# Modulation columns moved between the products of one token tile, first-layer splits moved to GpSimd, one subtraction moved in the recurrence

## The chip, the cores and the metric

The kernel runs on one core of a Trainium2 chip. The metric is the device time of one launch in microseconds (us). Time before: median 1755.17 us of three runs, 1753.87 to 1757.62.

## The reference

Two blocks of two layers each, on 512 tokens of width 1024, all in float32:

```python
def first_block(x, c, ...):
    c_act = jax.nn.silu(c)
    for i in range(DEPTH):                      # 2
        mods = jnp.split(c_act @ w_ada[i] + b_ada[i], 6, axis=-1)
        sh1, sc1, g1, sh2, sc2, g2 = [m[:, None, :] for m in mods]
        u = x * (1.0 + sc1) + sh1
        y = gla_mixer(...) if i % 2 == 0 else chunk_attention(...)
        x = layer_norm(DEEPNORM_ALPHA * x + (1.0 + g1) * y, ln_g[i, 0], ln_b[i, 0])
        u = x * (1.0 + sc2) + sh2
        y = squared_relu_mlp(u, ff_w1[i], ff_w2[i])      # square(relu(u @ w1)) @ w2, inner width 4096
        x = layer_norm(DEEPNORM_ALPHA * x + (1.0 + g2) * y, ln_g[i, 1], ln_b[i, 1])
    return x

def second_block(x, c, ...):
    cond = jax.nn.silu(c)
    for l in range(DEPTH):                      # 2
        mod = cond @ ada_w[l] + ada_b[l]
        shift, scale, gate = jnp.split(mod, 3, axis=-1)
        h = rms_norm(x, norm_g[l]) * (1.0 + scale[:, None, :]) + shift[:, None, :]
        y = even_mixer(...) if l % 2 == 0 else odd_mixer(...)
        x = x + gate[:, None, :] * y
    return x
```

The modulation of each block (`c_act @ w_ada`, `cond @ ada_w`) is computed from the vector `c` while the layers before it run. `even_mixer` begins with a product with `even_w_in`, then runs a recurrence with four heads (`hgrn2_chunked`) beside a pooled branch.

## The kernel before

**Products.** Each float32 operand is held as a high part (rounded to fp32r) and a low part (the rest), and each product is three matmuls: high by high, high by low, low by high (`PASSES`; `pe_tile`, L234, for the products with the transposed input `xT`; `down_tile`, L538, for the second feed-forward product). `xT[:, 0]` is the high part of the input, `xT[:, 1]` the low part. A half panel of weights (4 blocks of 128 rows by 512 columns) is loaded into `raw` by SyncE (SP), rounded into the high part by ScalarE (`act_high`, L191 and L192), and the low part is subtracted by GpSimd (`low`, L2595), block by block. PE waits for each block of the low part (`low_ready`).

**The token stream.** Tokens are in four tiles of 128. At a stage's end VectorE (DVE) mixes product, gate and residual for a tile; ScalarE normalises it; PE turns it (transposes, `pe_transposes_by_tile`, L375) into 8 PSUM banks; ScalarE writes `u` and the high part of `xT` (L416, L417); DVE subtracts the low part (`dve_split_x`, L423).

**The start.** DVE multiplies and adds `w_ada` in four groups of eight pieces (`first_tile`, L2716 and L2718) as SP brings them. After each group PE adds up the columns (`pe_first_columns`, L310 and L312), and ScalarE writes two blocks of `xT` with them. PE therefore takes the first panel block by block: products of block k, and after k = 0, 2, 4 the turning of the next two blocks of `x` (`pe_first_x`, L298) and their columns. DVE's splits of blocks 0 to 5 stand between its `first_tile` pieces; 6 and 7 stand behind them. `pe_at_work` (L304) is a run of matmuls whose result nobody reads.

**The end of the second feed-forward (`pe_ff`, `dve_ff` with l = 1).** The last two inner blocks are done as a pair (`down_pair`): output columns 0 to 511 (n = 0) into banks 4 to 7, then columns 512 to 1023 (n = 1) into banks 0 to 3, tile by tile, each tile with twelve matmuls of `hT` and twelve of `xT`. The modulation of the second block is ready in `modacc` by then, spread over partitions; it is added up by PE: as rows (`pe_modrow`, L776, for the two gates) or as columns (`pe_modcols`, L770: one matmul with one output column per 128 entries; the trace shows two records for each). In n = 1, tile 0, columns 0 to 15 stand one by one ahead of the first sixteen of the 24 matmuls. Columns 24 to 39 stand behind the rows, after the last product. On DVE `add_pair(n, t)` is add the earlier sum (L703), gate (L704), residual (L705), statistics (L819); a tile that was settled before (`settle`, L691 and L692: gate and residual of the earlier sum) skips the add. Ahead of the first tile of n = 1 stands `before_pair`: it waits for the columns (`mod_done` at 9) and makes the scale and shift of the next stage (L2758, L2781 to L2783). Behind the four tiles stand L2758 for columns 24 to 39 and `next_rows` (L2776, four pieces), and then `mod_made` goes to 9. PE turns banks 0 to 2 ahead (tiles 0 to 2), does three idle matmuls (L384), turns tile 3 of blocks 0 to 2, and waits for `mod_made` at 9 before it touches bank 3, which holds columns 24 to 39, and banks 4 to 7, which hold the rows.

**The recurrence (`hgrn_dve`).** One loop over 28 + 3 steps on DVE: `diff(t)` prepares an exponent for ScalarE (L2306, L2307), `take`, `gate`, `scaled(t - 1)` uses it (L2317, L2318), and at every sixth step `ends`, `states` (seven short dependent instructions, L2355 and L2357) and `written`.

The order on every engine is the order of the code; semaphores tie the engines together.

## Time and profile before

| | |
|---|---|
| median of three runs | 1755.17 us |
| the profiled execution, time | 1757.64 us |
| its span | 1755.8 us |
| granted TensorE clock, mean of the span | 0.995 |
| PE busy | 1739.7 us (99%) |
| PEld (weight load) busy | 1446.9 us (82%) |
| DVE busy | 1055.2 us (60%) |
| ACT busy | 765.2 us (44%) |
| POOL busy | 783.3 us (45%) |

Between the profiled execution's own time and its span lie 1.84 us. The chain of work that ended last runs on PE for 92% of the span, on DVE for 4%. Times within the span are given from its start. A row of the timeline has start, length, engine, line, operation, output and inputs, shapes, and count; in brackets the idle time of the engine before it and what ended it. Several like instructions are merged in a row; a matmul's end is modelled and reaches over the start of the next.

### The profile page before, as it was taken

To read this page: it belongs to the slowest core of one execution; us is meant where nothing else is said; L and a number is where in the kernel's file an instruction comes from. 1 tells how busy PE (TensorE), PEld (TensorE's weight loads), DVE (VectorE), ACT (ScalarE), POOL (GpSimd) and SP (SyncE) were. 2 spreads that over 40 slices of the span, in tenths; PEclk is the share of its full clock that TensorE was granted. 3 is DMA by queue.
4 is the path that set the end of the run, shared out by engine and by line. 5 is a ranking of instruction groups with operands and counts; after the bars stand their busy time and mean duration, and the time that the engine had idled before them with its cause. 6 is when DMAs were issued, how large, how long until landed. Compare 5 with 4: busy or idle time off the path is not lost.

```text
span 1755.8 us, 24977 instructions
## 1 busy us (share of the span) xinstructions
PE 1739.7 (99%) x9169; PEld 1446.9 (82%) x9169; DVE 1055.2 (60%) x1627; ACT 765.2 (44%) x1313; POOL 783.3 (45%) x610
## 2 busy tenths in 40 slices
PE   8999999999999999999999999999999999999999
PEld 7777788888888878888888888888888888888887
DVE  6887565666665862653465666659377844336752
ACT  3444445222222264663532222233545457666660
POOL 4524145555555464232355555553532344353342
PEclk9999999999999999999999999999999999999999
DMA  9744326645555233222285555541221122324521
GB/s 318 264 155 153 127 96 228 212 157 172 169 168 185 98 120 108 85 73 73 72 286 172 171 171 170 171 157 67 96 96 55 49 98 72 110 89 136 153 91 72
DMA packets 133884, 242.09 MB, mean 138 GB/s; under 512 B 6896, under 2 KB 44912, under 8 KB 133792
## 3 DMA queue, kind: packets, MB, share of 16 engines
q1 hardware_dynamic: 131616, 236.64, 41.4%
q10 hardware_dynamic: 2176, 4.19, 0.7%
q8 instruction: 61, 1.00, 0.2%
q14 instruction: 31, 0.25, 0.0%
HBM read 238.68 MB, written 2.13 MB: 137 GB/s over the span
## 4 chain that ended last, share of the span: by engine, by line
PE 92%; DVE 4%; DMA 1%; ACT 1%; issue 1%; SPq 0%; POOL 0%; DVEq 0%; POOLq 0%; ACTq 0%
PE bank L234 48%; PE bank L538 20%; PE bank L1536 5%; PE bank L1502 4%; PE bank L1504 3%; PE bank L1616 2%; PE bank L1604 2%; PE bank L1578 2%; DMA ring_s<-in_first_ada 1%; PE bank L2109 1%; PE bank L770 1%; PE bank L1095 0%; PE bank L1109 0%; DMA ct<-cumd 0%; PE bank L1840 0%
## 5 line engine op out<-in xcount | busy, mean ns | idle before, releaser
L2595 POOL TENSOR_TENSOR wsp<-raw,wsp 128x512 fp32r<-128x512 f32 x528 | 762.2, 1476 | 886.7 <-ACT wsp L191 886.7
L234 PE MATMUL bank<-xT,wsp 128*128 128x512 f32 x2592 | 601.5, 391 | 5.1 <-POOL wsp L2595 2.5
L234 PEld LDWEIGHTS bank<-xT,wsp 128*128 128x128 f32 x2592 | 486.2, 188 | 110.8 <-DVE xT L423 3.4
L191 ACT ACTIVATE wsp<-raw 128x1024 fp32r<-128x1024 f32 x132 | 139.8, 1059 | 485.6 <-PE bank L538 238.3
L538 PE MATMUL bank<-wsp,hT 128*128 128x512 f32 x1344 | 310.7, 390 | 0.0
L234 PE MATMUL bank<-wsp,xT 128*128 128x512 f32 x1248 | 299.4, 395 | 0.6 <-DVE xT L423 0.3
L538 PEld LDWEIGHTS bank<-wsp,hT 128*128 128x128 f32 x1344 | 252.3, 188 | 51.8
L234 PEld LDWEIGHTS bank<-wsp,xT 128*128 128x128 f32 x1248 | 230.7, 188 | 52.6 <-issue 4.9
L192 ACT ACTIVATE wsp<-raw 128x1024 fp32r<-128x1024 f32 x132 | 138.1, 1046 | 0.0
L685 DVE TENSOR_TENSOR x<-bank,x 128x512 f32<-128x512 f32 x80 | 55.0, 688 | 100.0 <-PE bank L538 100.0
L763 DVE SCALAR_TENSOR_TENSOR modacc<-ada_ring,csil,modacc 128x768 f32<-128x768 f32 (+1 forms) x80 | 99.4, 1243 | 4.0 <-DMA ada_ring<-in_ada_w 0.5
L669 DVE TENSOR_TENSOR hT<-h,hT 128x512 fp32r<-128x512 f32 x56 | 80.1, 1488 | 24.7 <-ACT hT L619 24.7
L1502 PE MATMUL bank<-xT,wsp 128*128 128x512 f32 x384 | 93.6, 397 | 0.0
L658 DVE TENSOR_TENSOR h<-bank,h 128x512 f32<-128x512 f32 x64 | 43.3, 687 | 75.7 <-ACT h L614 75.7
L614 ACT ACTIVATE h<-bank 128x512 f32<-128x512 f32 x64 | 38.3, 599 | 112.9 <-PE bank L234 112.9
L423 DVE TENSOR_TENSOR xT<-u,xT 128x512 fp32r<-128x512 f32 x64 | 53.7, 848 | 55.4 <-ACT xT L417 54.9
L1502 PEld LDWEIGHTS bank<-xT,wsp 128*128 128x128 f32 x384 | 70.4, 188 | 16.1 <-issue 2.0
L1709 DVE CUSTOM_DVE_ANT_0 aP<-bank,abt 128x512 f32<-128x512 f32 (+3 forms) x64 | 27.0, 487 | 69.4 <-PE bank L1578 59.8
L763 DVE SCALAR_TENSOR_TENSOR tok<-ring,csil,tok 128x512 f32<-128x512 f32 x56 | 54.9, 980 | 9.8 <-DMA ring<-in_w_ada 4.5
L763 DVE SCALAR_TENSOR_TENSOR modacc<-u,csil,modacc 128x768 f32<-128x768 f32 (+1 forms) x32 | 52.9, 1652 | 2.4 <-DVE modacc L763 0.5
L1504 PE MATMUL bank<-wsp,xT 128*128 128x256 f32 x384 | 48.0, 285 | 0.0
L1504 PEld LDWEIGHTS bank<-wsp,xT 128*128 128x128 f32 x384 | 46.5, 192 | 0.7 <-issue 0.7
(330 smaller groups left out, 2029.8 us busy)
## 6 DMA issues: line engine op xcount, KB each, us to landing
raw<-in_ff_w SPq DMA_DIRECT2D x64, 1024.0 KB, 5.4
ada_ring<-in_w_ada SPq DMA_DIRECT2D x48, 384.0 KB, 3.8
ada_ring<-in_ada_w SPq DMA_DIRECT2D x48, 384.0 KB, 3.7
ring<-in_w_ada SPq DMA_DIRECT2D x64, 256.0 KB, 3.1
raw<-in_odd_w_in SPq DMA_DIRECT2D x16, 1024.0 KB, 5.5
raw<-in_gla_w_in SPq DMA_DIRECT2D x12, 1024.0 KB, 6.7
raw<-in_att_w_in SPq DMA_DIRECT2D x12, 1024.0 KB, 5.2
raw<-in_even_w_in SPq DMA_DIRECT2D x12, 1024.0 KB, 5.2
```

What stands on the lines that cost most here:

```text
L191: act.activation(wsp[:, slot, 0, 0:HK // 2], raw[:, slot, 0:HK // 2], ACT.Copy).then_inc(hi_part, 1)
L192: act.activation(wsp[:, slot, 0, HK // 2:HK], raw[:, slot, HK // 2:HK], ACT.Copy).then_inc(hi_made, 1)
L234: mm = pe.matmul(out_ap, l, r, start=(start and n == 0), stop=(stop and n == 2))
L423: dve.tensor_tensor(xT[:, 1, k], u32[:, k % 2], xT[:, 0, k].bitcast(F32), ALU.subtract)\
L538: mm = pe.matmul(bank[bk][:, :], h[:, a, k, t * P:t * P + P], wsp[:, slot, c, k, :], start=(start and k == 0 and q == 0), stop=(stop and k ...
L669: dve.tensor_tensor(h[:, 1, t], h32[l][:, t], h[:, 0, t].bitcast(F32), ALU.subtract)\
L685: ins = dve.tensor_tensor(y, bank[4 + t][:, :], y, ALU.add)
L763: ins = dve.scalar_tensor_tensor(acc, w, c, acc, ALU.mult, ALU.add)
L1502: mm = pe.matmul(bank[D_BANK][:, :], w[:, i * P:i * P + P], xT[:, a, k, :], start=start, stop=stop)
L1504: mm = pe.matmul(bank[D_BANK][:, side:side + COLS // 2], xT[:, a, k, i * P:i * P + P], w, start=start, stop=stop)
L1536: mm = pe.matmul(bank[4 * n + t][:, :], (o_hi, o_lo)[a][name][:, kk, t * P:t * P + P], wsp[:, h, b, k, :], start=(kk == 0 and q == 0), sto ...
L2595: ins = pool.tensor_tensor(wsp[:, slot, 1, k], raw[:, slot, k], wsp[:, slot, 0, k].bitcast(F32), ALU.subtract)
```

## The change

1. The modulation columns 24 to 39 of the second feed-forward's end go from behind the rows to between the products of n = 1, tile 0: twelve matmuls of `hT` now carry columns 0 to 15, twelve of `xT` carry columns 24 to 39, one or two ahead of each. One signal (`mod_done`) stands behind the last of them. DVE takes both sets in `before_pair`.
2. PE turns four blocks ahead (k = 0 to 3) there, with eight idle matmuls, where it was three and three.
3. DVE settles tiles 3, 2 and 1 between its four squares, where it settled tile 3 behind its modulation pieces; `add_pair(1, 1)` and `add_pair(1, 2)` lose their add.
4. At the start the splits of `xT` blocks 0 to 5 go from DVE to GpSimd, between its low parts of the weights. For blocks 0 and 1 PE does all eight matmuls with the high part first, then the four with the low part.
5. `pe_at_work` 24 becomes 30, 6 becomes 10, 3 and 2, with waits for the first weights' high part and for `u` of block 0 between.
6. In the recurrence `diff(13)`, `diff(19)` and `diff(25)` stand one step earlier, ahead of `states`.

```diff
@@ -533,8 +533,8 @@
                         low_ready(pe, j, k)
                     for q, (a, c) in enumerate(PASSES):
                         n = 3 * k + q
-                        if n < len(columns):
-                            pe_modcols(pe, modacc[l], columns[n:n + 1], ST, mod_done if columns[n] == 15 else None)
+                        if columns:
+                            pe_modcols(pe, modacc[l], columns[n::3 * HK], ST, mod_done if columns[n] == 35 else None)
                         mm = pe.matmul(bank[bk][:, :], h[:, a, k, t * P:t * P + P], wsp[:, slot, c, k, :],
                                        start=(start and k == 0 and q == 0), stop=(stop and k == HK - 1 and q == 2))
                 return mm
@@ -577,7 +577,7 @@
                         if q == 0:
                             pe.wait_ge(s["ada_used"], KT * FB)
                             pe.wait_ge(s["acc_done"], 8 * i + 1)
-                        columns = (range(12), range(12, 16))[q]
+                        columns = (range(16), range(24, 40))[q]
                     mm = down_tile((hT[l], xT)[q], j + 2 + q, q, t, t, q == 0, q == 1, columns)
                     if t == ST - 1:
                         mm.then_inc(w_used, 1)
@@ -597,8 +597,6 @@
                 pe.wait_ge(s["acc_done"], 8 * (FB - 2) + 2 * r + 2)
                 pe_modrow(pe, modacc[l], off, ST + 2 * r, mod_done)
             pe.wait_ge(s["acc_done"], 8 * (FB - 2) + 2 * ST)
-            if l:
-                pe_modcols(pe, modacc[l], range(24, 40), HK - 1, mod_done, at=SEQ - P)
 
         def act_ff(act, l):
             s = FS[f"ff{l}"]
@@ -740,16 +738,20 @@
             for i in range(ST + 1, FB - 2):
                 step(i)
             ada(FB - 1, range(0, 4))
-            square(FB - 1)
+            for t in range(ST):
+                square(FB - 1, [t])
+                if affine and t < ST - 1:
+                    settle(1, ST - 1 - t)
             low(FB - 1, xT)
             ada(FB - 1, range(4, 8))
-            settle(1, ST - 1)
+            if not affine:
+                settle(1, ST - 1)
             for t in range(ST):
                 add_pair(0, t)
             for t in range(ST):
                 if t == (0 if affine else 2):
                     before_pair()
-                add_pair(1, t, t == ST - 1)
+                add_pair(1, t, t == ST - 1 or affine and t > 0)
                 if affine:
                     affine(t)
 
@@ -1114,7 +1116,15 @@
             for k in range(KT):
                 low_ready(pe, base["gla_in"] + k // HK, k % HK)
                 pe.wait_ge(free, k + 1)
-                for t in range(ST):
+                if k < 2:
+                    for a in range(2):
+                        if a:
+                            pe.wait_ge(ts["xT_ready"], ts["k0"] + k + 1)
+                        for t in range(ST):
+                            for b in range(2 - a):
+                                mm = pe.matmul(bank[t][:, :], wsp[:, 0, b, k, t * P:t * P + P], xT[:, a, k, :],
+                                               start=(k == 0 and a == 0 and b == 0), stop=False)
+                for t in range(ST if k >= 2 else 0):
                     mm = pe_tile(pe, bank[t][:, :], k // HK, k % HK, k, t, "T", k == 0, k == KT - 1,
                                  (ts["xT_ready"], ts["k0"] + k + 1) if t == 0 else None)
                     if k == KT - 1 and t < ST - 1:
@@ -2394,7 +2404,7 @@
                 dve.tensor_tensor(y, y, hu[:, t], ALU.mult).then_inc(s["pout"], 1)
 
             for t in range(NI + 3):
-                if t < NI and scaled_number(t) is not None:
+                if t < NI and scaled_number(t) is not None and not (t > 12 and t % 6 == 1):
                     diff(t)
                 if t >= 3:
                     take(t - 3)
@@ -2408,6 +2418,8 @@
                 if t >= 6 and t % 6 == 0 and t // 6 <= 4:
                     ends(t // 6 - 1)
                 if t >= 12 and t % 6 == 0:
+                    if t + 1 < NI:
+                        diff(t + 1)
                     states(t // 6 - 2)
                 if t >= 18 and t % 6 == 0:
                     written(t // 6 - 3)
@@ -2594,8 +2606,32 @@
                         pool.wait_ge(hi_made, 2 * i + slot + 1)
                     ins = pool.tensor_tensor(wsp[:, slot, 1, k], raw[:, slot, k], wsp[:, slot, 0, k].bitcast(F32), ALU.subtract)
                     ins.then_inc(lo_part if k < HK - 1 else lo_made, 1)
+            def low_of(slot, k):
+
+                ins = pool.tensor_tensor(wsp[:, slot, 1, k], raw[:, slot, k], wsp[:, slot, 0, k].bitcast(F32), ALU.subtract)
+                ins.then_inc(lo_part if k < HK - 1 else lo_made, 1)
+
+            def split_x(k):
+
+                ts = TS["in_gla_in"]
+                pool.wait_ge(ts["u_made"], ts["k0"] + k + 1)
+                pool.wait_ge(ts["bank_free"], k + 1)
+                pool.tensor_tensor(xT[:, 1, k], u32[:, k % 2], xT[:, 0, k].bitcast(F32), ALU.subtract).then_inc(ts["xT_ready"], 1)
+
+            pool.wait_ge(hi_made, 1)
+            for k in range(HK):
+                low_of(0, k)
+                if k < 2:
+                    split_x(k)
+            for k in (2, 3):
+                split_x(k)
+            pool.wait_ge(hi_made, 2)
+            for k in range(HK):
+                low_of(1, k)
+                if k < 2:
+                    split_x(HK + k)
             first = base["odd_in"] // 2 + PHASE0["odd_in"]
-            with pool.Fori(0, first) as i:
+            with pool.Fori(1, first) as i:
                 for slot in range(2):
                     low(i, slot)
             low(first, 0)
@@ -2675,11 +2711,15 @@
             for t in range(NV):
                 mm = pe.transpose(bank[0][:, t * P:t * P + P], vrow[:, t, :], ident[:, :])
             mm.then_inc(vtr_done, 1)
-            pe_at_work(pe, 24)
+            pe_at_work(pe, 30)
             pe.wait_ge(cols_made, 1)
             pe_first_x(pe, 0)
             pe_first_columns(pe, 0)
-            pe_at_work(pe, 6)
+            pe_at_work(pe, 10)
+            pe.wait_ge(hi_made, 1)
+            pe_at_work(pe, 3)
+            pe.wait_ge(TS["in_gla_in"]["u_made"], TS["in_gla_in"]["k0"] + 1)
+            pe_at_work(pe, 2)
             gla_pe(pe)
             pe_panels(pe, "gla_out", "mid_gla_out", [("NN", 1)], begin=pe_first_half_gla)
             pe_transposes_by_tile(pe, "hid_ff0", 2, KT - 1, idle=8)
@@ -2690,7 +2730,7 @@
             pe_out(pe, a_sem, "att_out")
             pe_transposes_by_tile(pe, "hid_ff1", 1, KT - 1, idle=8)
             pe_ff(pe, 1)
-            pe_transposes_by_tile(pe, "in_even_in", 1, HK - 1, lambda: pe.wait_ge(mod_made, 9), idle=3)
+            pe_transposes_by_tile(pe, "in_even_in", 1, HK, lambda: pe.wait_ge(mod_made, 9), idle=8)
             pe_panels(pe, "even_in", "in_even_in", [("TT", 1)])
             hgrn_pe(pe)
             pe_transposes_hgrn(pe, range(KT - 1))
@@ -2725,11 +2765,8 @@
             for g in range(HK):
                 for k in range(KT):
                     first_tile(g, k)
-                    if g and k == 3:
-                        dve_split_x(dve, "in_gla_in", 2 * g - 2)
-                    elif g and k == 5:
-                        dve_split_x(dve, "in_gla_in", 2 * g - 1)
             dve.sem_inc(mod_made, 1)
+            dve.wait_ge(TS["in_gla_in"]["xT_ready"], TS["in_gla_in"]["k0"] + KT - 2)
             for k in range(KT - 2, KT):
                 dve_split_x(dve, "in_gla_in", k)
 
@@ -2816,6 +2853,7 @@
 
             def before_pair1():
                 next_columns(0, ST, col("ada_b_2", 0, 16), 9)
+                next_columns(24, ST, col("ada_b_2", 24, 16), 9)
                 rms_fold(0)
                 dve.sem_inc(mod_made, 1)
                 dve.wait_ge(ln_ld, 128)
@@ -2827,7 +2865,6 @@
                 dve.scalar_tensor_tensor(x[:, t], tok[:, t], rstd[:, t:t + 1], lnrow[1][:, 1], ALU.mult, ALU.add)\
                    .then_inc(RS["even_in"]["x"], 1)
             dve_ff(dve, 1, KT, DEPTH, gate2, 96, before_pair1, affine1)
-            next_columns(24, HK - 1, col("ada_b_2", 24, 16), 12, SEQ - P)
             next_rows(1, 0.0, 10)
             dve.sem_inc(x_new, 1)
             dve_transposed(dve, "in_even_in")
```

The end of the second feed-forward on PE; L538 are products, L776 the rows, L770 the columns, L375 turns, L384 idle matmuls, L234 the next stage's products. Before:

```order
L538 MATMUL bank<-wsp,xT 128x512 x12
L776 MATMUL bank<-modacc,ones 128x512 x4
L770 MATMUL bank<-ones,modacc 128x1 x16
L375 MATMUL bank<-ident,tok 128x128 x9
L384 MATMUL bank<-ident 128x128 x3
L375 MATMUL bank<-ident,tok 128x128 x23
L234 MATMUL bank<-xT,wsp 128x512 x192
```

And now (L778 the rows):

```order
L538 MATMUL bank<-wsp,xT 128x512 x12
L778 MATMUL bank<-modacc,ones 128x512 x4
L375 MATMUL bank<-ident,tok 128x128 x12
L384 MATMUL bank<-ident 128x128 x8
L375 MATMUL bank<-ident,tok 128x128 x20
L234 MATMUL bank<-xT,wsp 128x512 x192
```

The sixteen columns are gone from here, three more turns are ahead, and five more idle matmuls.

The last squares of the second feed-forward on DVE (the squares write `h_1`, L669 are low parts, L763 modulation pieces, L691 and L692 one settled tile). Before:

```order
L658 TENSOR_TENSOR h_1<-bank,h_1 128x512 x4
L669 TENSOR_TENSOR xT<-h_1,xT 128x512 x4
L763 SCALAR_TENSOR_TENSOR modacc<-ada_ring,csil,modacc 128x2x384 x3
L763 SCALAR_TENSOR_TENSOR modacc<-u,csil,modacc 128x2x384
L691 TENSOR_TENSOR x<-x,gate 128x512
L692 SCALAR_TENSOR_TENSOR tok<-tok,x 128x512
L703 TENSOR_TENSOR bank<-bank,x 128x512
```

And now, from the third square on (L656; the squares before it are followed by the same two settling instructions; L667 are the low parts):

```order
L656 TENSOR_TENSOR h_1<-bank,h_1 128x512
L689 TENSOR_TENSOR x<-x,gate 128x512
L690 SCALAR_TENSOR_TENSOR tok<-tok,x 128x512
L656 TENSOR_TENSOR h_1<-bank,h_1 128x512
L667 TENSOR_TENSOR xT<-h_1,xT 128x512 x4
L765 SCALAR_TENSOR_TENSOR modacc<-ada_ring,csil,modacc 128x2x384 x3
L765 SCALAR_TENSOR_TENSOR modacc<-u,csil,modacc 128x2x384
L701 TENSOR_TENSOR bank<-bank,x 128x512
```

The settling stands between the squares, and four instructions more of it than before.

The start on GpSimd, behind its constants (`gAT` is the last of these). Before, the low parts of the weights stand in one loop (L2595); now the first two halves are written out, with the splits of `xT` (L2619) between:

```order
L2599 MEMSET gAT 128x1024
L2611 TENSOR_TENSOR wsp<-raw,wsp 128x512
L2619 TENSOR_TENSOR xT<-u,xT 128x512
L2611 TENSOR_TENSOR wsp<-raw,wsp 128x512
L2619 TENSOR_TENSOR xT<-u,xT 128x512
L2611 TENSOR_TENSOR wsp<-raw,wsp 128x512 x2
L2619 TENSOR_TENSOR xT<-u,xT 128x512 x2
L2611 TENSOR_TENSOR wsp<-raw,wsp 128x512
```

After these come the split of block 4, one low part, the split of block 5, and two low parts.

## Rows read from the trace of the kernel before

**Rows 1.** Page, section 1: busy time and share of the span.

```profile
PE 1739.7 (99%) x9169; PEld 1446.9 (82%) x9169; DVE 1055.2 (60%) x1627; ACT 765.2 (44%) x1313; POOL 783.3 (45%) x610
```

**Rows 2.** PE's waits: in total, times, longest, in us.

```profile
PE bank L375 <- DVEq L2777: 0.8, 2, 0.5
...
PE bank L2109 <- DVE hX L2318: 0.2, 1, 0.2
```

**Rows 3.** Timeline of PE at the start.

```profile
18.59 0.70 PE L234 MATMUL bank<-xT,wsp 128*128 128x512 f32 x2 [2.50 <-POOL wsp L2595]
20.39 4.63 PE L234 MATMUL bank<-xT,wsp 128*128 128x512 f32 x10 [1.09 <-DVE xT L423]
...
40.90 1.03 PE L298 MATMUL bank<-ident,x 128*128 128x128 f32 x8
...
43.26 8.45 PE L234 MATMUL bank<-xT,wsp 128*128 128x512 f32 x36
```

**Rows 4.** Single microseconds: length, PE busy (records), granted clock, DMA share, GB/s.

```profile
19.00:20.00 1.00, 0.30 (x2) 0.71 1.08 359
...
26.00:27.00 1.00, 1.00 (x11) 0.88 1.10 366
```

**Rows 5.** Timeline of DVE at the start: first and last piece of group 3.

```profile
34.33 0.75 DVE L2716 TENSOR_SCALAR bank<-ring_s,csil 128x512 f32<-128x512 f32 x1 [0.59 <-DMA ring_s<-in_first_ada]
...
41.32 0.75 DVE L2718 SCALAR_TENSOR_TENSOR tok<-ring_s,csil,bank 128x512 f32<-128x512 f32 x1
```

**Rows 6.** Timeline at the start: ACT and weight load of block 4.

```profile
32.98 1.06 ACT L191 ACTIVATE wsp<-raw 128x1024 fp32r<-128x1024 f32 x1 [2.32 <-DMA raw<-in_gla_w_in]
...
36.06 0.77 ACT L417 ACTIVATE xT<-bank,ctmp 128x512 fp32r<-128x512 f32 x1
...
38.49 2.14 PEld L234 LDWEIGHTS bank<-xT,wsp 128*128 128x128 f32 x10 [0.53 <-DVE xT L423]
```

**Rows 7.** Timeline of POOL at the start: low parts of the second half panel.

```profile
34.11 5.48 POOL L2595 TENSOR_TENSOR wsp<-raw,wsp 128x512 fp32r<-128x512 f32 x4 [12.64 <-ACT wsp L191]
```

**Rows 8.** Timeline of PE at the second feed-forward's end.

```profile
1200.59 0.48 PE L538 MATMUL bank<-wsp,xT 128*128 128x512 f32 x1
...
1201.04 2.33 PE L538 MATMUL bank<-wsp,xT 128*128 128x512 f32 x9
...
1219.53 3.59 PE L776 MATMUL bank<-modacc,ones 128*128 128x512 f32 x8
1222.96 3.63 PE L770 MATMUL bank<-ones,modacc 128*128 128x1 f32 x32
1226.45 1.18 PE L375 MATMUL bank<-ident,tok 128*128 128x128 f32 x9
1227.47 1.24 PE L384 MATMUL bank<-ident 128*128 128x128 f32 x6
...
1229.82 3.03 PE L375 MATMUL bank<-ident,tok 128*128 128x128 f32 x20 [0.47 <-DVEq L2777]
```

**Rows 9.** Timeline of DVE over the same stretch and the squares ahead of it.

```profile
1170.45 0.69 DVE L658 TENSOR_TENSOR h<-bank,h 128x512 f32<-128x512 f32 x1 [2.03 <-ACT h L614]
...
1186.65 1.77 DVE L691 TENSOR_TENSOR x<-x,gate 128x512 f32<-128x512 f32 x1
...
1201.83 0.17 DVE L2758 TENSOR_TENSOR modcol<-bank,cols 128x16 f32<-128x16 f32 x1
...
1203.47 0.70 DVE L703 TENSOR_TENSOR bank<-bank,x 128x512 f32<-128x512 f32 x1 [0.87 <-PE bank L538]
...
1224.49 1.28 DVE L2827 SCALAR_TENSOR_TENSOR x<-tok,rstd,lnrow 128x1024 f32<-128x1024 f32 x1
1226.63 0.17 DVE L2758 TENSOR_TENSOR modcol<-bank,cols 128x16 f32<-128x16 f32 x1 [0.85 <-PE bank L770]
1226.84 2.87 DVE L2776 SCALAR_TENSOR_TENSOR gate<-bank,brow 128x512 f32<-128x512 f32 x4
```

**Rows 10.** The chain that ended last: start, us, what.

```profile
1172.50 21.76 PE bank L538 x96
```

## The prediction

> **What bounds the kernel now.** I read the busy times first: PE is busy for 1739.7 of the span's 1755.8 us [rows 1], so all that better order can win anywhere is PE's 16 us of idle time, and part of those is the unavoidable start. Then PE's waits: the start, one wait of 0.5 us for DVE at the end of the second feed-forward, and 0.2 us in the recurrence [rows 2]. So only three places can matter, and I read the timelines of these. At the start the reader is to see that PE begins block 0 at 18.59, waits 1.09 us for a low part, then needs 4.63 us for ten matmuls [rows 3] because the granted clock has fallen to its lower level, 1.2 GHz, by 20 and comes back during 26 to 27 [rows 4]; yet the DMA share is over 1.0 there and DVE's last group starts only at 34.33, on a DMA [rows 4, 5]. At the end of the second feed-forward PE goes through products, rows, columns, turns and idle matmuls with one gap of 0.47 us, while DVE runs a serial tail that ends in the rows' gates [rows 8, 9].
>
> **The start: DVE loses six splits, GpSimd gets them.** DVE's group 3 runs from 34.33 to 42.07 [rows 5]: 7.74 us for eight pieces and two splits. A piece lasts 0.75; with what lies between two of them eight take about 6.6, so without the splits the group ends at 41.0, 1.1 earlier. That is what the columns of group 3, and so all that PE does from 43.26 on, could win at most. But PE must also get there earlier, and its block 4 hangs on other things. The second half of the first weights lands at 32.98; ACT rounds it for 2 us, then writes `u` and the high part of block 4, which is there at 36.06 + 0.77 = 36.83 [rows 6]. Neither moves: the DMA engines are full to the brim [rows 4]. Then block 4's low part: DVE had it at about 38.49 [rows 6]. GpSimd takes 5.48 / 4 = 1.37 us for such a piece beside DVE [rows 7]; its low part of weights block (1, 0) starts after ACT's second rounding at 35.0 and ends at 36.4, so the split runs from 36.9 to 38.25. PE goes on at 38.25 instead of 38.49, takes ten matmuls and 2.4 us, reaches the turning at 40.65 where it stood at 40.90 [rows 3], and no longer has to wait for DVE's last piece. Block 5's split ends at 41.0 and is needed at 43; weights (1, 3) end at 43.8 and are needed at 48; blocks 6 and 7 stay on DVE, which gets something to split only after PE's columns (43) and so never waits for GpSimd's six (41.0); behind that wait stand its constants and the next modulation pieces. **Term 1: -0.45 us.** Bounds: +0.4 if each GpSimd piece takes 1.77 us (below) instead of 1.37, and -1.2 if block 4 is not late at all.
>
> The queues that it passes: SP's loads into `raw` wait for GpSimd's low parts, which end some 4 us later in each half (two or three splits of 1.37 stand between them), but the next half panels stand on SP behind modulation pieces that wait for DVE, so nothing is late. GpSimd's own loop starts one round later with nothing waiting.
>
> **The padding.** 30, 10, 3 and 2 instead of 24 and 6: a call takes some 0.34 us at this shape (three calls in 1.24 us less the last one's modelled tail [rows 8]) and less in a long run. PE then starts block 0 near 19.5 to 20 instead of 18.59, but at the full 2.4 GHz: twelve matmuls in 2.7 us end at 22.5, not at 25. Blocks 1 to 3, which need the columns of groups 1 and 2 and `x` on its DMAs, then run up to about 35.3 and PE stands before block 4 until 36.85, and again for its low part until 38.25. **Term 2: 0**, since the wait for block 4 swallows it; bounds: the clock rival below, and its mirror.
>
> **Order of the matmuls of blocks 0 and 1.** Eight matmuls cover the 1.09 us wait [rows 3]. It lies ahead of the same block 4: 0.
>
> **Columns 24 to 39.** An interleaved column makes a matmul's pitch 0.45 instead of 21.76 / 96 = 0.227 us [rows 8, 10], so it costs 0.22 to 0.23; at the tail sixteen took 1226.45 - 1222.96 = 3.49, or 0.22 each [rows 8]. PE's sum is therefore the same: +3.6 in tile 0, -3.5 behind the rows. But they now stand ahead of DVE's tail. Tile 0 of n = 1 ended at 1201.04 + 2.33 = 1203.37 and will end at 1207.0; the last column (35) is through 0.35 earlier, one matmul before the end, at 1206.65. Only then does `before_pair` run, which was hidden in a wait of 0.87 [rows 9]: five small instructions at 0.2, so `add_pair(1, 0)` begins at 1207.65, 4.2 later than 1203.47. Behind the waiting instruction on DVE stands its whole tail, and ACT's and PE's last tile behind that.
>
> **Settling.** It removes one add (0.70) each for tiles 1 and 2 from the tail, which ran from 1203.47 to 1224.49 + 1.28 = 1225.77, 22.3 us; it becomes 20.9 and ends at 1228.55. The settling itself goes into the gaps of 2.03 us between squares [rows 9]: two instructions of 0.70, 1.4 to 1.5 in all, fit. At worst both take 1.77, as L691 did beside GpSimd [rows 9]; then a square comes 1.5 late, and the low parts behind it, which PE needs at the half of the pair's first 96 matmuls, 1172.50 + 10.9 = 1183.4 [rows 10], while DVE has done them and four modulation pieces besides by 1186.65. 0, bound +1. What went from behind the modulation pieces (L691 and L692 there, 3.4 us) leaves DVE free to be earlier in n = 0, and it then waits for tile 0.
>
> The Trainium skill, SBUF — State Buffer, section "Who interferes with whom", says that a DVE instruction with two SBUF inputs contends with a GpSimd one that reads SBUF, and that the second one to issue blocks until the first is done. The trace agrees: L691 with both inputs in SBUF takes 1.77 beside GpSimd, L703 with one in PSUM 0.70 [rows 9]. By this rule alone the settling could cost up to the full bound just given; for GpSimd's new splits it speaks of no loss beside `first_tile`, whose sum lies in PSUM.
>
> **Behind the tail.** `next_rows` started at 1226.84, because L2758 had to wait for the columns [rows 9]; now it starts at 1228.55, lasts 2.87 and lets PE past at 1231.5, 1.7 later than 1229.82. PE then has 16 turns left instead of 20, 2.4 us instead of 3.03, and ends them at 1233.9 instead of 1232.85 [rows 8]: +1.1. PE's own sum gives nearly the same: the rows start at 1219.53 + 3.6 = 1223.1 and take 3.4, 12 turns at 0.11 (nine in 1227.47 - 1226.45) 1.4, eight idle calls at 0.34 2.7, 20 turns 3.0: 1233.7, or +0.9. So either way **term 3: +1.1 us**, bounds +0.7 and +1.6. Nothing behind it can take it back: PE has no wait of size until the end [rows 2].
>
> **The recurrence.** `diff` before `states` gives ACT its exponent 3 us earlier, but `scaled` stands where it was in DVE's row, and PE's waits there are 0.2 and less [rows 2]. **Term 4: -0.15**, bounds 0 and -0.4.
>
> **The sum.** -0.45 + 1.1 - 0.15 = +0.5 us. Against the profiled execution's 1757.64 that is 1758.1; this execution lies 2.5 above the median of the runs, so for a median I put the same 0.5 on 1755.17: 1755.7.
>
> **The rivals.**
>
> *The clock falls at block 4 (slower).* Before, PE idled for 2.50 us ahead of 18.59, then did little, and the clock went down for about 6.8 us, from 19.4 to 26.2 [rows 3, 4]. Now PE stands for 1.55 us at 35.3 and 1.0 us at 37.3. If the clock falls there, it falls where PE is the bound: 6.8 us at half speed lose 3.4. With the rest: +3.9, 1759.1. It decides when the idle share around 35 to 38 is as large as it was at 16 to 19. For it: the two gaps add up to 2.6. Against: PE is busy in front of them and between. The Trainium skill, TensorE: Matmul & The Clock Gate, section "What's actually happening", says that the throttled state is the default and that activity releases it; the trace agrees at 26, and it names this risk without pricing it.
>
> *The clock fall of before costs more in other executions (faster).* In the profiled one the 6.8 us at half clock lay in the shadow of block 4. PE had 0.53 us of slack there [rows 6]; where the fall comes a few us later, up to 3.4 us of it are on PE's path, and the padding takes them away. Then the median would be 2 to 3 lower: 1753. For it: the runs of before spread over 3.75 us. Against: nothing shows that the spread lies there.
>
> *Two columns in one gap cost no more than one (faster).* Then tile 0 gets 1.8 longer instead of 3.6 and the tail of DVE ends 1.8 earlier: 1754. Against: at the tail, where nothing separates them, each still costs 0.22 [rows 8], and PE's own sum with the five more idle calls caps the gain.
>
> *The splits on GpSimd do not relieve the start.* At 1.77 us a piece PE resumes block 4 at 38.9: 1756.5.
>
> **How the numbers follow.** Chances: forecast 0.55; clock falls at block 4 0.13; before's fall was worth more 0.17; cheap pairs 0.07; GpSimd late 0.08. A measurement here can hardly tell less than 0.2%, 3.5 us, from none. Faster by more (below 1751.7) needs the third case at its largest plus the best bounds: 0.09. Slower by more (above 1758.7) is most of the clock case and a little of spread: 0.13. Within: 0.78. The range takes in the clock rival's 1759.1, at the lower end the 1753 of the other one less some spread of a median of few runs (the runs of before lie up to 2.5 from theirs): 1752.3 to 1759.3.
>
> **What would show it.** In the changed kernel's profile: PE's products from block 5 on (before 43.26) start 0.2 to 0.8 earlier; clock 1.0 through 19 to 26; gaps of 1 to 1.6 us ahead of block 4 and for its low part; DVE's first add of tile 0 in n = 1 near 1207.2 after an idle stretch of 8 us (all times less term 1); `next_rows` ends near 1231; the turns end near 1233.4. I am wrong if the DVE tail does not start some 4 us later, if the turns end before 1232.85, or if the clock is below 1.0 anywhere between 28 and 50.

## The result, and the profile after

The changed kernel takes 1760.25 us (median of 20 executions, 1755.24 to 1764.87); the kernel before, timed beside it on the same chip, 1756.09 (20 executions, 1753.23 to 1758.95). The ratio is 1.0018, 95% interval 1.0010 to 1.0026. The ratio is not that of the two medians, which is 1.0024 (4.2 us). So the change costs 3 to 4 us; the forecast was +0.5 us, with 1759.3 as the upper end of the range. Carried over to the 1755.17 of the runs before, the ratio gives 1758.3: inside the range and on the slow side of it. The profiled execution took 1760.59 us, its span is 1758.9.

The page's first section, as in [rows 1]:

```profile
PE 1744.4 (99%) x9209; PEld 1451.3 (83%) x9209; DVE 1053.4 (60%) x1623; ACT 764.1 (43%) x1313; POOL 790.2 (45%) x616
```

PE is still busy for 99% of the span, but for 4.7 us more than before. PE's longest releaser among its waits at the second feed-forward's end is now ScalarE's `tok` and no longer DVE's gates (in total, times, longest):

```profile
PE bank L375 <- ACT tok L845: 1.3, 2, 1.1
```

**The start**, as in [rows 3] (timeline of PE: start, length, instruction; the wait before it in brackets):

```profile
14.32 3.99 PE L304 MATMUL bank<-ident 128*128 128x128 f32 x30
18.36 3.00 PE L1125 MATMUL bank<-xT,wsp 128*128 128x512 f32 x12
22.64 1.09 PE L298 MATMUL bank<-ident,x 128*128 128x128 f32 x8 [1.29 <-DMA x<-in_x]
...
24.61 4.58 PE L1125 MATMUL bank<-xT,wsp 128*128 128x512 f32 x12
...
33.69 6.14 PE L234 MATMUL bank<-xT,wsp 128*128 128x512 f32 x24
...
41.58 4.80 PE L234 MATMUL bank<-xT,wsp 128*128 128x512 f32 x20
```

The 15 idle calls (30 records) fill 14.32 to 18.3, the first block follows in 3.0 us without a break, there is no wait ahead of block 4 (inside the 24 matmuls from 33.69), and block 5's products begin at 41.58, 1.68 us earlier than at 43.26. DVE's group 3, to be held against [rows 5]:

```profile
33.58 0.75 DVE L2756 TENSOR_SCALAR bank<-ring_s,csil 128x512 f32<-128x512 f32 x1 [2.86 <-DMA ring_s<-in_first_ada]
...
39.58 0.75 DVE L2758 SCALAR_TENSOR_TENSOR tok<-ring_s,csil,bank 128x512 f32<-128x512 f32 x1
```

The group begins 0.75 us earlier, since its DMA landed earlier, and lasts 40.33 - 33.58 = 6.75 us instead of 7.74: 1.74 together, about PE's 1.68.

**The clock.** Stretches of the changed kernel: length, then PE, PEld, DVE, ACT and POOL busy with records, then the granted clock, DMA share and GB/s (the columns of [rows 4] with all engines):

```profile
19.00:26.00 7.00, 5.71 (x33) 4.67 (x32) 5.20 (x8) 1.68 (x4) 5.59 (x5) 0.91 1.07 379
24.00:28.00 4.00, 4.00 (x15) 3.31 (x15) 3.58 (x5) 2.96 (x5) 1.60 (x2) 0.59 1.07 374
28.00:50.00 22.00, 21.89 (x114) 18.17 (x113) 13.62 (x21) 11.20 (x17) 11.33 (x10) 1.00 0.80 277
...
1202.00:1209.00 7.00, 7.00 (x26) 6.00 (x25) 1.25 (x6) 0.00 (x0) 0.00 (x0) 0.52 0.21 83
```

There is still a fall in the start, later and shorter than in [rows 4]; from 28 to 50 the clock is full. But there is a new fall in 1202 to 1209, and PE is busy there for 7.00 of 7 us.

**The end of the second feed-forward**, as in [rows 8]. L772 is the column matmul; the trace has two records of each call:

```profile
1192.52 0.50 PE L772 MATMUL bank<-ones,modacc 128*128 128x1 f32 x4
1192.88 0.49 PE L538 MATMUL bank<-wsp,hT 128*128 128x512 f32 x1
1193.20 0.50 PE L772 MATMUL bank<-ones,modacc 128*128 128x1 f32 x4
...
1201.58 0.28 PE L772 MATMUL bank<-ones,modacc 128*128 128x1 f32 x2
1201.72 0.48 PE L538 MATMUL bank<-wsp,xT 128*128 128x512 f32 x1
1202.04 0.28 PE L772 MATMUL bank<-ones,modacc 128*128 128x1 f32 x2
...
1203.45 0.42 PE L772 MATMUL bank<-ones,modacc 128*128 128x1 f32 x2
1203.73 0.77 PE L538 MATMUL bank<-wsp,xT 128*128 128x512 f32 x1
1204.30 0.42 PE L772 MATMUL bank<-ones,modacc 128*128 128x1 f32 x2
...
1224.76 3.59 PE L778 MATMUL bank<-modacc,ones 128*128 128x512 f32 x8
1228.19 1.47 PE L375 MATMUL bank<-ident,tok 128*128 128x128 f32 x12
1229.50 1.95 PE L384 MATMUL bank<-ident 128*128 128x128 f32 x16
1232.51 2.64 PE L375 MATMUL bank<-ident,tok 128*128 128x128 f32 x20 [1.06 <-ACT tok L845]
1234.91 5.27 PE L234 MATMUL bank<-xT,wsp 128*128 128x512 f32 x21
```

To 1202 a gap with two columns and its product have a pitch of 0.68 us (1192.52 to 1193.20) and one with one column 0.46 (1201.58 to 1202.04), as forecast. From 1202.3 on the clock is at its lower level, and the gap with one column has 0.85 (1203.45 to 1204.30). Tile 0 thereby ends at 1207.7. PE's first product of the next stage, at 1234.91, stands 42.39 us behind the first column; before it was 1232.60 - 1194.10 = 38.50. DVE, as in [rows 9]:

```profile
1164.04 1.59 DVE L689 TENSOR_TENSOR x<-x,gate 128x512 f32<-128x512 f32 x1
1165.66 1.66 DVE L690 SCALAR_TENSOR_TENSOR tok<-tok,x 128x512 f32<-128x512 f32 x1
...
1168.68 0.69 DVE L690 SCALAR_TENSOR_TENSOR tok<-tok,x 128x512 f32<-128x512 f32 x1
...
1207.39 0.38 DVE L2795 TENSOR_TENSOR modcol<-bank,cols 128x16 f32<-128x16 f32 x2 [11.20 <-PE bank L772]
...
1208.61 0.70 DVE L701 TENSOR_TENSOR bank<-bank,x 128x512 f32<-128x512 f32 x1 [0.23 <-DVE bcol L2820]
...
1228.77 1.28 DVE L2865 SCALAR_TENSOR_TENSOR x<-tok,rstd,lnrow 128x1024 f32<-128x1024 f32 x1
1229.97 2.13 DVE L2813 SCALAR_TENSOR_TENSOR gate<-bank,brow 128x512 f32<-128x512 f32 x3
```

The first two settling instructions take 1.6 us each beside GpSimd's low parts (1161.28 to 1166.77), the later ones 0.69. Then DVE is idle for 11.20 us until the columns are there, begins its first add of tile 0 at 1208.61 and ends the tail at 1230.05.

### The profile page after: what moved, and what is told of

It reads as the page before. It is cut to its first block, busy times and chain, and to the rows that moved or that the text cites. A ratio compares the mean times of both kernels' runs of the same rounds, so it can differ in the third digit from the quotient of the medians.

```text
span 1758.9 us, 24938 instructions
## 1 busy us (share of the span) xinstructions
PE 1744.4 (99%) x9209; PEld 1451.3 (83%) x9209; DVE 1053.4 (60%) x1623; ACT 764.1 (43%) x1313; POOL 790.2 (45%) x616
## 4 chain that ended last, share of the span: by engine, by line
PE 92%; DVE 3%; DMA 2%; ACT 2%; issue 1%; SPq 0%; POOL 0%; DVEq 0%; POOLq 0%; ACTq 0%
PE bank L234 49%; PE bank L538 20%; PE bank L1546 5%; PE bank L1512 4%; PE bank L1514 3%; PE bank L1626 2%; PE bank L1614 2%; PE bank L1588 2%; PE bank L2119 1%; DMA x<-in_x 1%; PE bank L772 1%; DMA raw<-in_gla_w_in 1%; PE bank L1097 0%; DVE fP L1719 0%; DMA ct<-cumd 0%
## 5 line engine op out<-in xcount | busy, mean ns | idle before, releaser
L2607 POOL TENSOR_TENSOR wsp<-raw,wsp 128x512 fp32r<-128x512 f32 x520 | 751.4, 1477 | 867.8 <-ACT wsp L191 867.8
L234 PE MATMUL bank<-xT,wsp 128*128 128x512 f32 x2568 | 593.7, 390 | 1.6 <-ACT xT L417 1.3
L234 PEld LDWEIGHTS bank<-xT,wsp 128*128 128x128 f32 x2568 | 480.4, 188 | 105.9 <-issue 2.9
L538 PE MATMUL bank<-wsp,hT 128*128 128x512 f32 x1344 | 311.6, 391 | 0.0
L234 PE MATMUL bank<-wsp,xT 128*128 128x512 f32 x1248 | 299.5, 395 | 0.6 <-DVE xT L423 0.3
L538 PEld LDWEIGHTS bank<-wsp,hT 128*128 128x128 f32 x1344 | 252.9, 188 | 52.1
L234 PEld LDWEIGHTS bank<-wsp,xT 128*128 128x128 f32 x1248 | 230.7, 188 | 52.6 <-issue 4.9
L667 DVE TENSOR_TENSOR hT<-h,hT 128x512 fp32r<-128x512 f32 x56 | 80.1, 1488 | 24.7 <-ACT hT L617 24.7
L1512 PE MATMUL bank<-xT,wsp 128*128 128x512 f32 x384 | 93.6, 396 | 0.0
L656 DVE TENSOR_TENSOR h<-bank,h 128x512 f32<-128x512 f32 x64 | 43.4, 688 | 69.8 <-ACT h L612 69.8
L1512 PEld LDWEIGHTS bank<-xT,wsp 128*128 128x128 f32 x384 | 70.4, 188 | 16.1 <-issue 2.0
L423 DVE TENSOR_TENSOR xT<-u,xT 128x512 fp32r<-128x512 f32 x58 | 49.5, 862 | 54.1 <-ACT xT L417 53.6
L538 PE MATMUL bank<-wsp,xT 128*128 128x512 f32 x192 | 49.7, 405 | 0.0
```

The lines of the kernel that those rows point to most:

```text
L234: mm = pe.matmul(out_ap, l, r, start=(start and n == 0), stop=(stop and n == 2))
L423: dve.tensor_tensor(xT[:, 1, k], u32[:, k % 2], xT[:, 0, k].bitcast(F32), ALU.subtract)\
L538: mm = pe.matmul(bank[bk][:, :], h[:, a, k, t * P:t * P + P], wsp[:, slot, c, k, :], start=(start and k == 0 and q == 0), stop=(stop and k ...
L667: dve.tensor_tensor(h[:, 1, t], h32[l][:, t], h[:, 0, t].bitcast(F32), ALU.subtract)\
L1512: mm = pe.matmul(bank[D_BANK][:, :], w[:, i * P:i * P + P], xT[:, a, k, :], start=start, stop=stop)
L2607: ins = pool.tensor_tensor(wsp[:, slot, 1, k], raw[:, slot, k], wsp[:, slot, 0, k].bitcast(F32), ALU.subtract)
```

## The experiments

All were timed beside the kernel before, in three sessions. The medians below stand beside those of before in the same session: 1756.97 for e1b, e2b, e3b and e4b, 1756.13 for h1, h2, g1 and g2, 1756.48 for i1, i2, i3 and i4. Kernels of different sessions are best compared by their ratios to before. Intervals are of 95%. The mean granted clock is given over all executions of a kernel; before's is 0.9961 (0.9959 to 0.9964 by session), that of after 0.9963.

Two readings serve all of them. ScalarE runs the same 1779 instructions in the same order in every one of these kernels, so the start of its instruction number n tells at any place how much later one profiled execution is than another. And the trace gives each stretch in which the clock was at its lower level (0.5). The table shows, for each profiled execution, what a section adds against that of before, in us, and the stretches of lower clock, in us of the span (a last one at the very end of the span is left out):

```
                 start  layer-0  ff1 end  recur-  rest   sum   clock at 0.5
                 <103   columns           rence
before            0      0        0        0       0      0    19.4-26.2  807.9-814.7  1227.7-1231.1
after            -1.68   0.01     4.11    -0.45    0.97   3.04 24.8-28.2  806.4-813.2  1202.3-1209.2
e1 columns       -0.87  -1.64     2.73    -0.06    0.97   1.26 13.9-24.2  809.2-812.6
e2 no columns    -1.91  -1.61    -0.33    -0.45    0.22  -3.97            806.6-810.0  1223.0-1226.4
e3 start          1.27  -1.60    -0.33    -0.04    0.46  -0.28 24.6-31.4  809.7-813.1  1226.1-1229.5
e4 thin          -1.00  -1.62     1.09    -0.46    1.98   0.02            808.1-811.6
h1 wide          -1.93  -1.64     1.33    -0.45   -0.03  -2.65            807.8-811.2
i1 narrow        -2.07  -1.62     5.69    -0.46    0.97   2.55            807.4-810.8  1199.9-1210.2
h2 best          -1.83  -3.19    -0.59    -0.45    0.89  -5.14 23.9-27.3
i2 both wide     -1.54  -3.19     1.30    -0.47    0.34  -3.57
i3 before wide   -0.17  -3.19    -0.59    -0.02    0.30  -3.68 13.9-24.2
g1 padding       -0.01   0.00    -0.07     0.00    0.42   0.36            807.8-814.6  1227.6-1231.1
g2 splits        -0.30  -1.64    -0.04     0.01   -0.11  -2.04 14.0-24.3  809.4-812.8  1225.8-1229.2
i4 settle         0.27  -1.63    -0.12    -0.45    0.54  -1.38 14.4-17.8, 21.2-24.6  809.7-813.1  1226.1-1229.5
```

The sections are, by the times of ScalarE's instructions in before: up to 103.2 us; 800.8 to 816.3; 1195.3 to 1265.6; from there to 1447.2; and the rest. What the stretches between them add is under 0.15 us and counts in the sum only. The column "rest" (from 1447 on) goes from -0.1 to 2.0 and follows no edit. It goes with one wait, PE's for DVE's `fP` (L1604 of before): 0.4 us in all in before and in the five kernels with a rest of -0.1 to 0.34, 0.6 to 0.8 where it is 0.4 to 0.5, 1.0 to 1.7 where it is 0.9 to 2.0. What makes DVE late there was not tested. One profiled execution is one sample: these numbers say where, the medians say how much.

**e1b_columns: the columns alone** (before with parts 1 and 2):

```
...
-                        columns = (range(12), range(12, 16))[q]
+                        columns = (range(16), range(24, 40))[q]
...
-            if l:
-                pe_modcols(pe, modacc[l], range(24, 40), HK - 1, mod_done, at=SEQ - P)
...
-            pe_transposes_by_tile(pe, "in_even_in", 1, HK - 1, lambda: pe.wait_ge(mod_made, 9), idle=3)
+            pe_transposes_by_tile(pe, "in_even_in", 1, HK, lambda: pe.wait_ge(mod_made, 9), idle=8)
```

> The kernel before with only the columns, turns and idle matmuls changed (parts 1 and 2). Clock theory (one-column matmuls one or two to a gap bring the granted clock down inside tile 0, 0.50 from about 10 us after its start, for some 6.8 us): +1.1 from the later tail and up to +3.4 from the clock, so +3 to +4.5 us over before, and the profile shows 0.5 between 8 and 17 us after the first column. Late tail theory (only DVE's tail starts later): +1.1 us, clock 1.0 through tile 0, or a fall there as often as in before.

1762.76 us (6 executions), ratio 1.0037 (1.0025 to 1.0049), mean clock 0.9943. The columns cost, and more than the whole change; more, too, than either theory expected (+3 to +4.5, or +1.1). What the rest of the change gives back is missing here: 2.0 us of the start (e3b) and 1.4 of the settling (below), together with after's 3.2 about the 6.5 that the ratio says. The profiled execution is the fastest of the six (1758.84; the others go to 1766.23 with a clock of 0.992). It has no fall in tile 0, so what the clock theory expected to see there is not seen in this trace; its end of the feed-forward is +2.73 all the same: with the settling left out, the tail of DVE is late by more.

**e2b_no_columns: everything but the columns** (after, parts 1 and 2 taken back, the diff above reversed):

> The changed kernel without parts 1 and 2 (columns and turns as before; start, settling and recurrence changed). Clock theory: the start's gain stands alone, -1 to -2 us against before, no 0.5 in tile 0 of the second feed-forward's end. Late tail theory: the same sign, -1.5; both expect about 4 to 5 and 2.6 us less than the changed kernel, respectively.

1754.59 us (11), ratio 0.9989 (0.9981 to 0.9998), mean clock 0.9980. Without parts 1 and 2 the change is faster than before. Next stage's first product:

```profile
1228.80 11.46 PE L234 MATMUL bank<-xT,wsp 128*128 128x512 f32 x49
```

It comes 38.11 us behind the first column, against 42.39 in after.

**e3b_start: parts 4 and 5 alone** (the splits and the order of blocks 0 and 1, and the padding):

> The kernel before with only the start changed (parts 4 and 5). My prediction had -0.45; the profile of the changed kernel shows block 5 begin 1.68 us earlier (41.58 against 43.26). If the profile's difference is the start's own, the median is 1.0 to 1.8 us under before, and equals the run without columns within 0.5 (settling and recurrence worth nothing).

1754.96 us (11), ratio 0.9988 (0.9979 to 0.9997), mean clock 0.9977. Practically all that e2b gains is gained here, a little more than the 1.0 to 1.8 us expected; what settling and the recurrence add is too small to be timed. The profiled execution is the slowest of the eleven, so its +1.27 in the start stands for itself alone.

**e4b_thin: the second sixteen columns spread over tiles 1 and 2**, one ahead of every third matmul, in bank 5, with columns 0 to 15 of tile 0 as before:

```
...
-                        columns = (range(16), range(24, 40))[q]
+                        columns = (range(12), range(12, 16))[q]
+                    elif l and t < 3:
+                        at = 24 + 4 * (2 * (t - 1) + q)
+                        pe.wait_ge(s["acc_done"], 8 * i + 2)
+                        columns = range(at, at + 4)
...
```

> The changed kernel, but tile 0 carries its sixteen columns 0 to 15 as before, and columns 24 to 39 stand one ahead of every third matmul of tiles 1 and 2, in bank 5; DVE takes them after tile 2. Same PE work and same end of the products. Clock theory: the matmul stream is thinned less, no fall of the clock there, so 2 to 3.4 us less than the changed kernel (near before, -0.5 to +0.5). Late tail theory: DVE may start tile 0 3.6 us earlier but waits for tile 3's products anyway, so within 1 us of the changed kernel.

1757.21 us (11), ratio 1.0000 (0.9992 to 1.0009), mean clock 0.9980. The same sixteen calls, thinly spread, are 3 us cheaper than dense in tile 0, with a fuller clock. That points to the clock, but it also moves the calls off DVE's way. The next two kernels differ in nothing but the width of these calls.

**h1_wide and i1_narrow: the same order, 128 columns or one.** A column matmul needs one output column. In h1_wide it writes 128, of which the next call overwrites all but one:

```
-                mm = pe.matmul(bank[bk][:, at + b:at + b + 1], acc[:, a:a + P], ones[:, 0:1], start=True, stop=True)
+                mm = pe.matmul(bank[bk][:, at + b:at + b + wide], acc[:, a:a + P], ones[:, 0:wide], start=True, stop=True)
...
-                            pe_modcols(pe, modacc[l], columns[n::3 * HK], ST, mod_done if columns[n] == 35 else None)
+                            bs = columns[2 * n:2 * n + 2] if n < 4 else columns[n + 4:n + 5]
+                            pe_modcols(pe, modacc[l], bs, ST, mod_done if bs[-1] == 39 else None, wide=P)
```

> The kernel after, but each of the 32 column matmuls in tile 0 writes 128 columns of bank 4 instead of one (its own sum and 127 spare ones, which the next calls and nobody's reads cover), in ascending order; everything else as after. The array is streamed through for as many columns as in a small product, and one call of 128 columns lasts as long as one of one column (0.22 us: 8 calls of the tail in 1.75 us in the trace). Theory A (one-column calls among the products bring the clock down in tile 0): the granted clock stays at 1.0 from 1192 to 1210, the pairs keep their pitch of 0.69 us, and the whole is 3.4 us shorter than after in the executions where after falls, so about 1757 us, ratio to before 1.0005. Theory B (the fall has nothing to do with what the columns are like, it comes of the gaps, the loads of fp32 weights or by chance of the position): the fall stays in 1202 to 1209 and the time at 1760. In both, the stage after the first feed-forward starts no earlier than 38.9 us behind its first column.

i1_narrow is this kernel without the `wide=P`:

> The kernel after with its columns in ascending order, as in the wide one, but one column wide as in after: the control for the wide one. Theory A (the width of the calls decides): the clock falls to 0.5 for 3.4 or 6.8 us between 1195 and 1210 again, and the time is that of after, 1759 to 1761 us, ratio 1.0018 or more. Theory B (the order of the columns, or which gap holds two, decided): it is as fast as the wide one, 1756 us, ratio 1.000.

Wide: 1756.13 us (11), ratio 1.0001 (0.9992 to 1.0011), mean clock 0.9985. Narrow: 1760.43 us (12), ratio 1.0024 (1.0012 to 1.0036), mean clock 0.9960. Stretches of the wide one, then of the narrow one (columns as above; the granted clock is the third number from the end):

```profile
804.00:811.00 7.00, 7.00 (x44) 6.33 (x44) 4.28 (x12) 3.47 (x10) 1.64 (x2) 0.77 0.43 150
1202.00:1209.00 7.00, 7.00 (x36) 5.88 (x35) 5.17 (x12) 0.41 (x2) 0.00 (x0) 1.00 0.00 0
```

```profile
1195.00:1202.00 7.00, 7.00 (x45) 6.43 (x43) 0.00 (x0) 0.00 (x0) 1.85 (x2) 0.85 0.45 152
1202.00:1209.00 7.00, 7.00 (x22) 5.84 (x23) 2.95 (x8) 0.00 (x0) 0.00 (x0) 0.50 0.00 0
```

With PE busy for 7.00 of 7 us in both, the clock is 1.00 with wide calls and 0.50 with narrow ones. The pitch is the same: PE's timeline in h1_wide has

```profile
1190.60 0.61 PE L773 MATMUL bank<-ones,modacc 128*128 128x128 f32 x4
1190.97 0.48 PE L539 MATMUL bank<-wsp,hT 128*128 128x512 f32 x1
1191.28 0.60 PE L773 MATMUL bank<-ones,modacc 128*128 128x128 f32 x4
...
1201.90 0.38 PE L773 MATMUL bank<-ones,modacc 128*128 128x128 f32 x2
1202.04 0.48 PE L539 MATMUL bank<-wsp,xT 128*128 128x512 f32 x1
1202.35 0.38 PE L773 MATMUL bank<-ones,modacc 128*128 128x128 f32 x2
...
1230.21 10.03 PE L234 MATMUL bank<-xT,wsp 128*128 128x512 f32 x42
```

The pair and its product have 0.68 us (1190.60 to 1191.28), the single 0.45 (1201.90 to 1202.35), as one-column calls have at full clock. So 127 columns of waste cost nothing and save 4.0 us by the ratios (1.0024 - 1.0001), or 3.0 against after; by the medians 4.3 and 4.1. The mean clocks say the same: 0.9985 - 0.9960 = 0.0025 of 1757 us is 4.4 us lost. Nor does it rest on two traces: among the twenty executions of after the two at a clock of 1.000 take 1755.2 and 1755.4 us, the three at 0.993 take 1764.2 to 1764.9, a straight line fitted through all gives 1.3 us for each 0.001, and i1's twelve give 1.6, from 1753.94 to 1766.38. The executions of after spread over 9.6 us and those of i1 over 12.4, those of h1 over 3.0. In layer 0, where h1 has its calls as before (16 in a row), its clock still falls: 0.77 in 804 to 811.

**g1_padding and g2_splits: the two parts of the start, each alone.** g1 is before with part 5, g2 before with part 4:

```
-            pe_at_work(pe, 24)
+            pe_at_work(pe, 30)
...
-            pe_at_work(pe, 6)
+            pe_at_work(pe, 10)
+            pe.wait_ge(hi_made, 1)
+            pe_at_work(pe, 3)
+            pe.wait_ge(TS["in_gla_in"]["u_made"], TS["in_gla_in"]["k0"] + 1)
+            pe_at_work(pe, 2)
```

> Before with part 5 alone (the idle transposes of the start: 30, 10, 3, 2 with the two waits among them). My sum for the padding was 0. Theory A (the gain of the start is that the clock falls there less often): the median takes most of what parts 4 and 5 together took, ratio 0.999 (1755.3), with a mean clock of 0.997 to 0.998 over the executions against 0.996 of before, while an execution at full clock takes as long as one of before (1751.7). Theory B (the gain of the start is the work taken from VectorE): no difference, ratio 1.000 within 0.0005.

> Before with part 4 alone (the splits of the first six transposed blocks on GpSimd, and the first two blocks' products in the new order), the padding as before. Term 1 of the prediction puts it at -0.45 us (ratio 0.9997). Theory A (padding makes the gain): ratio 1.000, clock falls as often as in before. Theory B (splits make the gain): ratio 0.999, products of block 5 start 1 to 1.7 us earlier than 43.26.

g1: 1756.24 us (11), 1.0004 (0.9995 to 1.0013), mean clock 0.9978. g2: 1755.51 us (11), 0.9999 (0.9990 to 1.0008), mean clock 0.9965. Neither alone shows the gain that both together have. g1's fall in the start is gone:

```profile
19.00:26.00 7.00, 5.69 (x33) 4.71 (x33) 6.48 (x10) 1.35 (x3) 2.31 (x2) 1.00 1.06 380
```

but PE still waits for DVE's split in block 4, as it did before:

```profile
37.09 2.56 PE L234 MATMUL bank<-xT,wsp 128*128 128x512 f32 x10 [0.95 <-DVE xT L423]
...
41.86 4.39 PE L234 MATMUL bank<-xT,wsp 128*128 128x512 f32 x18
```

and the 1.40 us that it is ahead at block 5 is given back by 103, at one place. DVE's last piece of the modulation (its weights are `ring`) waits for its DMA until 78.07, as in before (78.15); behind it on DVE stands the first layer's `gke`, and PE waits for that. DVE and PE in g1, then the same two in before:

```profile
78.07 0.75 DVE L763 SCALAR_TENSOR_TENSOR tok<-ring,csil,tok 128x512 f32<-128x512 f32 x1 [1.99 <-DMA ring<-in_w_ada]
...
89.37 0.65 PE L1072 MATMUL bank<-ident,gke 128*128 128x128 f32 x4 [1.14 <-DVE gke L1294]
```

```profile
78.15 0.75 DVE L763 SCALAR_TENSOR_TENSOR tok<-ring,csil,tok 128x512 f32<-128x512 f32 x1 [1.09 <-DMA ring<-in_w_ada]
...
89.47 0.60 PE L1072 MATMUL bank<-ident,gke 128*128 128x128 f32 x4
```

g2 is 1.27 us ahead at block 5, with its clock at the lower level from 14.0 to 24.3; there too PE then waits for `gke`, 0.75 us, and 0.30 are left at 103. Theory A of g1 falls in time though its clock did rise. The first half of g2's theory B came out in the trace (block 5 is 1.27 us earlier), but the time did not follow.

**i4_settle: parts 3 and 6 alone** (settling between the last squares; the difference ahead of the states):

> Before with part 3 (settling between the last squares) and part 6 (the difference ahead of the states) alone. The prediction's terms for them: settling takes 1.4 us from VectorE's tail, of which PE gets what its wait at the turns holds (bounds 0 and 1.1 us, since before's PE waits 1.06 us there for x), and the recurrence gives 0.15 us. Theory A (the tail gains, the recurrence gives 0.2): ratio 0.9993, 1 us less. Theory B (the wait only moves to the next releaser and GpSimd's shared time costs VectorE 2 us): ratio 0.9999 to 1.0002.

1756.17 us (11), ratio 1.0002 (0.9993 to 1.0010): nothing that can be timed, theory B. In the table the recurrence gains 0.45 us, here and in every kernel that has part 6 (0.45 to 0.47 in eight); in the others it moves by at most 0.06.

**i2_both_wide, h2_best and i3_before_wide.** i2 is h1_wide with wide calls in layer 0's attention stage too (L1639). h2 is e2b with wide calls at all three places: 128 in tile 0 and in layer 0, 64 at the tail. i3 is before with just those:

```
...
-                    pe_modcols(pe, modacc[0], range(24, 40), D_BANK, mod_done)
+                    pe_modcols(pe, modacc[0], range(24, 40), D_BANK, mod_done, wide=P)
...
-                pe_modcols(pe, modacc[l], range(24, 40), HK - 1, mod_done, at=SEQ - P)
+                pe_modcols(pe, modacc[l], range(24, 40), HK - 1, mod_done, at=SEQ - P, wide=64)
```

> After with wide columns in tile 0 and in layer 0's attention stage: the same clock as the kernel of both widths without parts 1 and 2 (ratio 0.9979), so the difference to that one is the price of parts 1 and 2 by themselves. Theory A (a late tail: first column to next stage 39.6 us against 37.9 in the two traces): 1.7 us longer than it, about 1754.3 us, ratio 0.999, mean clock 0.999 or more. Theory B (parts 1 and 2 cost nothing beside the clock): 1752.5 us, ratio 0.998.

> The kernel after without parts 1 and 2 (columns 24 to 39 at the tail again, four blocks turned behind the last rows, three idle calls), and every one-column matmul of the modulation of layers 0 and 1 made wide: 128 columns in tile 0 of the first feed-forward's end and in the attention stage of layer 0 (line 1639 of before, 16 calls in a row), 64 at the tail. Theory A (one-column calls bring the clock down): the fall at 804 to 811 us, which every trace so far has, goes, and with it 3.4 us; mean clock from 0.998 to 0.999 or 1.0; 1751 to 1752 us, ratio to before 0.997. Theory B (the fall at 804 comes of something else in that stage): the fall stays there, and the time is that of the kernel without the columns, 1754.6 us, ratio 0.999.

> Before with nothing but its one-column matmuls of the modulation made wide (128 columns in tile 0 and in layer 0's attention stage, 64 at the tail). Theory A: the falls at 804 to 811 us and at 1228 to 1231 us go, those of the start stay; by the falls that the other executions lose (about 1.2 us for each 0.001 of mean clock, and 0.003 of it), 1753.5 us, ratio 0.9983 to 0.9987. Theory B (wide calls help only with the rest of the change): ratio 0.9995 or more.

i2: 1754.01 us (11), 0.9988 (0.9979 to 0.9997), mean clock 0.9996. h2: 1752.55 us (11, 1752.02 to 1753.18), **0.9979 (0.9970 to 0.9988)**, mean clock 0.9996: it is faster than both kernels, and its executions lie within 1.2 us of each other. i3: 1754.15 us (11), 0.9989 (0.9980 to 0.9998), mean clock 0.9983. h2 and i3 stay a little short of what was expected of them (0.997, and 0.9983 to 0.9987), i2 is where its theory A put it. Stretches of h2 at the start, in layer 0, in tile 0 and at the tail:

```profile
24.00:28.00 4.00, 4.00 (x13) 3.29 (x14) 3.48 (x6) 2.96 (x5) 1.32 (x2) 0.59 1.07 374
...
804.00:811.00 7.00, 7.00 (x53) 6.46 (x52) 4.21 (x11) 3.53 (x10) 1.71 (x2) 1.00 0.40 150
1202.00:1209.00 7.00, 7.00 (x32) 5.79 (x32) 6.79 (x9) 3.23 (x9) 0.00 (x0) 1.00 0.00 0
1224.00:1232.00 8.00, 7.14 (x42) 6.28 (x43) 3.49 (x6) 8.00 (x13) 2.70 (x3) 1.00 0.40 131
```

The falls at 804 to 811 and at the tail, where calls stood sixteen in a row, are gone; one in the start is left. Each of the three kernels is 3.19 us shorter in the layer-0 section than before with its fall of 6.8 us, and those with a fall of 3.4 us are 1.6 shorter. i2 and h2 differ by parts 1 and 2 (and the width of 64 at h2's tail), at an equal clock: 1.5 us by the medians (0.0009 in ratio), 1.9 in the table.

## Why the prediction was right or wrong

**The verdict.** The time lies in the range, but +0.5 was too low: about +3 is near the upper edge, and the interval (0.10 to 0.26%) lies above zero, although I had written that less than 0.2% can hardly be told from none. That it lies in the range is partly luck. Two errors of opposite sign met: the start gave 1.5 us more than summed, and the clock took 3 to 4 us for which the sum over the columns had nothing. The upper end, 1759.3, was there for a fall of the clock at another place that had the same price.

**Term 1, the start (-0.45, bounds +0.4 and -1.2): mis-sized.** Seven kernels with parts 4 and 5 and a fall of at most 3.4 us in the start are 1.0 to 2.1 us ahead at 103 us (mean 1.7); the five without part 4 lie between -0.87 and +0.27 (mean -0.2, before's own 0 among them). So the two parts give 1.5 us in the traces and 2.0 by e3b's median, more than the bound of 1.2. DVE's group 3 shrank by 1.0 as worked out. The step that failed is "Neither moves": ScalarE's rounding and block 4's high part did move, by 0.8 and 1.1 us, since the DMAs landed earlier, and with them the limit that I had set at block 4. Much of that is not the change's: in e1b, g1 and i3 they moved too, so before's profiled execution had late DMAs, and I had treated its one landing time as fixed. The wait for GpSimd's split of block 4 was forecast rightly: in the five kernels with parts 4 and 5 and no fall of the clock in the start, PE waits 0.62 or 0.63 us for it and goes on at 36.72 to 37.41, where I had 38.25.

**Term 2, the padding (0): right by itself; beside part 4 it seems to be worth something.** g1 shows 1.0004 and -0.01 us. That kills the rival "the clock fall of before costs more" for the padding alone: there is no fall in the start of g1 and it gains nothing. (Block 0 itself began at 18.36, not at 19.5 to 20.) I had held that the wait at block 4 swallows what the padding wins. The trace shows otherwise: 1.40 us are won at block 5 and lost again at 89 us, where PE waits for DVE's `gke`. The prediction does not have this second limit, since before's PE comes there just as DVE is done (89.33 and 89.47) and so shows no wait. Of seven kernels with parts 4 and 5 and a short fall or none, six show no wait there, and e4b shows 0.69 us; it is the one with only 1.00 us left at 103. In the six DVE's last modulation piece of that stage begins at 76.3 at the latest, in g2 and g1 at 77.8 and 78.1. Why the two parts together take 2.0 us off (e3b) and neither alone does is therefore argued and not shown: the interval of e3b (0.9979 to 0.9997) overlaps those of g1 and g2 (from 0.9995 and 0.9990), and the places are read from single traces.

**The columns (+3.6 in tile 0, -3.5 behind): right.** A column costs 0.22 to 0.23 us, alone or in a pair; the rival of cheap pairs is dead.

**DVE's tail (4.2 later, 20.9 long): right at full clock.** In h1_wide, at full clock, the first add comes 13.9 us behind the first column, against 1203.47 - 1194.10 = 9.4 before: 4.5 later. It lasts from 1204.52 to 1225.34, 20.8.

**Settling (1.4 off the tail, 0 at the squares): right.** With the columns ahead of the tail it is worth 1.4 us (+2.73 in e1b without it, +1.33 in h1 with it); without them nothing (-0.12 in i4). By the Trainium skill, SBUF — State Buffer, section "Who interferes with whom", a DVE instruction with two SBUF inputs contends with a GpSimd one that reads SBUF: the trace agrees, 1.59 and 1.66 us beside GpSimd's pieces and 0.69 without them. So the second square came 1.2 us later behind the first than in before (3.92 against 2.72 us), the third 0.5; by the fourth, which waits for ScalarE again, 0.07 was left, and the low parts of the squares stand as far behind the first square as in before (10.57 and 10.58).

**Term 3 (+1.1, bounds +0.7 and +1.6): right where the clock is full.** h1 and i2 are 1.33 and 1.30 us later than before. Against h2 it is 1.9, because before's own end had a fall that costs it 0.6 (i3).

**Term 4 (-0.15, bounds 0 and -0.4): -0.45**, the right sign and just outside.

**The rival "the clock falls at block 4" (+3.9, 0.13): the price was right, the place and the cause were wrong, and so the chance.** I had tied it to idle gaps of PE at block 4. From 28 to 50 the clock was 1.00. It fell at 1202, among the columns and with PE busy throughout, where I had written "wrong if the clock is below 1.0 anywhere between 28 and 50" and had looked nowhere else. Its price at half speed, 3.4 us for 6.8, is about what is measured: 3.0 by the ratios of after and h1_wide, 4.0 by those of i1 and h1, and in the traces 4.11 - 1.33 = 2.8 for 6.8 us and 5.69 - 1.33 = 4.4 for 10.2. So the step that failed is the sum over the columns: I priced their time on PE and the lateness of DVE, and put the clock at nothing there, without a reason; it measured 3 to 4 us. The hint stood in the trace of before. At 805 us sixteen such calls in a row

```profile
805.16 4.53 PE L770 MATMUL bank<-ones,modacc 128*128 128x1 f32 x32
```

end at 809.7, and the clock is at its lower level from 807.9 to 814.7, with PE busy throughout; and again at 1227.7, 1.2 us behind the sixteen calls of [rows 8]. I had only looked at the clock at the start.

**The account by ratios.** e2b is 1.9 us below before; the late tail adds 1.6 (i2 against h2); the narrow calls in tile 0 add 3.0 (after against h1) or 4.0 (i1 against h1). The sum is +2.7 to +3.7, measured +3.2. Each ratio has an interval of about 1.6 us to either side, so the agreement is no closer than that. Open are why parts 4 and 5 gain only together, and what makes DVE late for `fP` behind 1447 us, up to 2 us between single executions.

## What to carry to other kernels

Price moved instructions by what they do to the clock too, not only by their time: here one-column matmuls were as long as those of 128 columns and kept PE busy, yet the clock went to half with them. Where the output has spare columns, try such calls 64 or 128 wide; that alone was worth 2 us here, as much as the whole gain of the start. Look at the granted clock over the whole span before predicting, and ask at each fall which instructions stood ahead of it. And where a gain at one place is to reach the end, look for the next place at which another engine is only just in time: it shows no wait before the change.

## What the runs showed of the hardware that was not expected

The granted clock fell to 0.5 with PE busy for 7.00 of 7 us, during or right behind fp32 matmuls of one output column. It fell with 16 of them in a row in all eleven profiled executions that had them in layer 0 (for 3.4 or 6.8 us) and in all six that had them at the tail (3.4 us), and with 32 among the products of tile 0 in two of three (6.8 and 10.2 us, not in e1b). With 16 among them, as in before, no fall was seen in tile 0. Made 128 wide, the calls take the same 0.22 to 0.23 us, and no fall was seen: not in tile 0 of h1 and i2 with 32 of them, not in layer 0 of i2, h2 and i3, and not at the tail of h2 and i3, where they are 64 wide. The Trainium skill, TensorE: Matmul & The Clock Gate, section "HAM oscillation — how this bites in real kernels", explains falls by idle gaps of PE that wait for DMA; here the trace does not agree, since PE was busy for 17.00 of the 17 us ahead of the fall in after (1185 to 1202), and two kernels alike but for the width of these calls had 0.50 and 1.00 in 1202 to 1209 us.
